# The feed-forward norm of an encoder block: roots on a diagonal, weights as ScalarE's scale, another order of the last sums

## The reference

```
mixed = concat([attention, convolution])
h  = h + mixed @ w_out[0]
hn = rmsnorm(h, ffn_norm_g)          # h * rsqrt(mean(h*h) + 1e-6) * g
g, u = hn @ w_gate, hn @ w_up        # 1024 -> 2816
h  = h + (silu(g) * u) @ w_down
out = rmsnorm(h, final_norm_g)[16:]
```

## Time and profile before

| | |
|---|---|
| runs | 1173.94, 1174.21, 1174.76 us; median 1174.21 |
| profiled execution | 1174.17 us |
| its span, first to last instruction | 1172.4 us |
| busy: TensorE, VectorE, POOL, ScalarE | 1151.2, 693.5, 451.2, 435.7 us |
| mean granted clock of TensorE | 0.998 |

### The profile page before, as it was taken

One profiled execution on the slowest core, in us unless ns is written; L12 is line 12 of the kernel. 1 busy time (PEld: TensorE's weight loads), 2 busy tenths in 40 slices (PEclk: granted clock), 3 DMA queues, 4 the chain that ended last, 5 costly groups with the idle time before them and its releaser, 6 DMA issues.

```text
span 1172.4 us, 15242 instructions
## 1 busy us (share of the span) xinstructions
PE 1151.2 (98%) x5890; PEld 986.8 (84%) x5890; DVE 693.5 (59%) x757; ACT 435.7 (37%) x875; POOL 451.2 (38%) x356
## 2 busy tenths in 40 slices
PE   9999999999999999989999999999999999999997
PEld 5899899899999888867888888888888888888886
DVE  5339898888898646694444445353435353534347
ACT  6321553533737644454141413132322222232323
POOL 4116000000000013267474646556564647473822
PEclk9999999999999999999999999999999999999999
DMA  7204312113026011122030202121212121212114
GB/s 265 81 10 100 71 48 72 38 49 85 13 54 227 19 37 54 36 72 62 13 102 5 87 22 73 36 72 36 72 37 72 37 72 36 72 37 72 37 36 162
DMA packets 70911, 75.69 MB, mean 65 GB/s; under 512 B 11513, under 2 KB 60149, under 8 KB 70840
## 3 DMA queue, kind: packets, MB, share of 16 engines
q1 hardware_dynamic: 69656, 72.60, 20.0%
q10 hardware_dynamic: 1184, 2.13, 0.5%
HBM read 64.13 MB, written 6.32 MB: 60 GB/s over the span
## 4 chain that ended last, share of the span: by engine, by line
PE 69%; DVE 5%; POOL 3%; issue 2%; ACT 0%; POOLq 0%; DVEq 0%; ACTq 0%
PE ps L1820 31%; PE ps L1841 20%; PE ps L1771 8%; PE ps L1631 6%; DVE gq L1298 3%; PE ps L1704 2%; POOL wa_lo L639 1%; DVE acc L1213 1%; PE ps L1689 1%; PE ps L1677 1%; POOL wb_lo L639 1%; DVE wo_lo L1236 0%; PE ps L1784 0%; PE ps L1754 0%; PE ps L1747 0%
## 5 line engine op out<-in xcount | busy, mean ns | idle before, releaser
L1486 DVE TENSOR_TENSOR mix<-ps,mix 128x512 f32<-128x512 f32 x176 | 121.7, 691 | 137.4 <-PE ps L1841 137.4
L1213 DVE SCALAR_TENSOR_TENSOR acc<-u_pad,par,acc 128x1024 f32<-128x1024 f32 x116 | 144.4, 1292 | 1.5 <-ACT acc L830 1.4
L1841 PE MATMUL ps<-wd_hi,act_hi 128*128 128x512 f32 x352 | 137.0, 389 | 0.3 <-DVE act_lo L1475 0.3
L1841 PE MATMUL ps<-wd_lo,act_hi 128*128 128x512 f32 x352 | 136.9, 389 | 0.0
L1841 PE MATMUL ps<-wd_hi,act_lo 128*128 128x512 f32 x352 | 136.9, 389 | 0.0
L625 POOL TENSOR_SCALAR ln_var<-bn 128x1 f32<-128x1 f32 x8 | 3.6, 450 | 338.7 <-DVE bn L1335 338.7
L1631 PE MATMUL ps<-hn_hi,wp_hi 128*128 128x348 f32 (+2 forms) x352 | 118.4, 336 | 0.0
L1631 PE MATMUL ps<-hn_lo,wp_hi 128*128 128x348 f32 (+2 forms) x352 | 117.6, 334 | 0.0
L1631 PE MATMUL ps<-hn_hi,wp_lo 128*128 128x348 f32 (+2 forms) x352 | 117.5, 334 | 0.0
L639 POOL TENSOR_TENSOR wa_lo<-raw,wa_hi 128x512 fp32r<-128x512 f32 x44 | 61.8, 1406 | 142.5 <-ACT wa_hi L1002 142.5
L1051 ACT ACTIVATE act_f<-ps 128x512 f32<-128x512 f32 x22 | 13.1, 598 | 246.1 <-PE ps L1820 246.1
(11 more groups left out here) (187 smaller groups left out, 2644.8 us busy)
## 6 DMA issues: line engine op xcount, KB each, us to landing
raw<-in_w_gate SPq DMA_DIRECT2D x11, 1024.0 KB, 5.3
raw<-in_w_up SPq DMA_DIRECT2D x11, 1024.0 KB, 5.3
wd_f<-in_w_down SPq DMA_DIRECT2D x11, 1024.0 KB, 4.8
raw<-in_w_in SPq DMA_DIRECT2D x16, 512.0 KB, 3.8
xin<-in_x SPq DMA_DIRECT2D x8, 512.0 KB, 10.4
wo_raw<-in_w_out SPq DMA_DIRECT2D x4, 1024.0 KB, 9.5
mix<-in_x SPq DMA_DIRECT2D x8, 512.0 KB, 3.4
out<-ost SPq DMA_DIRECT2D x7, 512.0 KB, 2.6
```

What stands on the lines that cost most here:

```text
L1213: dve.scalar_tensor_tensor(out=acc[:, j % 2, :], in0=u_pad[:, p % 2, j:j + L], scalar=par[:, p, j:j + 1], in1=acc[:, j % 2, :], op0=ALU.mu ...
L1486: dve.tensor_tensor(hrow, ps[:, TB + n % 4, :], hrow, ALU.add).then_inc(d_added, 1)
L1841: last = pe.matmul(ps[:, TB + n % 4, :], a[s][:, t, i * P:(i + 1) * P], w_[m][:, t, dh * BANK:(dh + 1) * BANK], start=(t == 0 and s == m = ...
```

## The change

POOL's `h_root(i)` now also multiplies the identity by the root of each token into `h_diag`, in two buffers. `transpose_h` multiplies the row of h itself, as stationary operand, by that diagonal: an f32 matmul for each block in place of a transpose. `norm_h` is gone. The weights of the norm lie in `g2c`, one column a block, and `evac_h` copies the banks in eight instructions with them as scale. `square_h` waits for its own last sum in place of the transposes. The slots 4 and 5 change places. `weight_sum(0,5)` and `weight_hi(0,5)` go ahead, to the last iteration of the tiles; `h_root(7)` goes ahead of the weight sums; `evac_h(7)` and `hi_h(7)` go ahead of `weight_hi(0,6)` and `(0,3)`, with `t_high` of T1 now ahead of all three; the sums T1 and T3 of tiles 6 and 7 alternate.

```diff
-             ("g2b", [P, D], F32)],
+             ("h_diag", [P, 2, P], F32)],
+        g2c = keep("g2c", [P, KD], F32)
-        FIRST_SLOT = [0, 1, 2, 0, 5, 2, 4, 0, 3, 5, 1, 2, 4, 3]
+        FIRST_SLOT = [0, 1, 2, 0, 4, 2, 5, 0, 3, 4, 1, 2, 5, 3]
-        SLOT = FIRST_SLOT + [(0, 5, 1, 2, 4, 3)[n % SLOTS] for n in range(len(LATER))]
+        SLOT = FIRST_SLOT + [(0, 4, 1, 2, 5, 3)[n % SLOTS] for n in range(len(LATER))]
-                  + [(t, i) for t in ("T1", "T3", "T2", "T4") for i in (6, 7)])
+                  + [(t, i) for i in (6, 7) for t in ("T1", "T3")] + [(t, i) for t in ("T2", "T4") for i in (6, 7)])
-            sp.dma_start(g2b[:, :], ffn_norm_g[0].partition_broadcast(P)).then_inc(g2_loaded, 16)
+            sp.dma_start(g2c[:, :], ffn_norm_g[0].rearrange("(k p) -> p k", p=P), allow_slow_non_contiguous=True).then_inc(g2_loaded, 16)
@@ POOL, h_root(i)
+                pool.wait_ge(h_rstd, i + 1)
+                if i >= 2:
+                    pool.wait_ge(ht_ready, i - 1)
+                pool.tensor_scalar(h_diag[:, i % 2, :], ident[:, :], rstd[:, n:n + 1], None, ALU.mult).then_inc(h_diag_ready, 1)
@@ POOL, loop over the tiles
+                if i == TILES - 1:
+                    pool.wait_ge(ms_used, TILES)
+                    weight_sum(0, 5)
                 if i >= 1:
                     h_root(i - 1)
@@ POOL, behind it
+            h_root(TILES - 1)
             pool.wait_ge(wo_ready, 2 * TILES)
-            weight_sum(0, 5)
             weight_sum(0, 6)
-            h_root(TILES - 1)
             weight_sum(0, 3)
@@ ScalarE
             def square_h(i):
                 act.wait_ge(h_ready, 2 * (i + 1))
                 if i:
-                    act.wait_ge(ht_ready, i)
+                    act.wait_ge(h_sumsq, i)
...
             def evac_h(i):
                 c = slice((i % 4) * P, (i % 4 + 1) * P)
+                if i == 0:
+                    act.wait_ge(g2_loaded, 16)
                 act.wait_ge(ht_ready, i + 1)
-                act.activation(hn2f[:, i // 4, :, c],
-                               ps[:, TB:TB + 2, :].rearrange("p b (k t) -> p (b k) t", k=4), ACT.Copy).then_inc(hf_ready, 1)
+                for k in range(KD):
+                    act.activation(hn2f[:, i // 4, k, c], ps[:, TB + k // KH, (k % KH) * P:(k % KH + 1) * P], ACT.Identity,
+                                   scale=g2c[:, k:k + 1], bias=zeros[:, 0:1]).then_inc((hf_low, hf_high)[k // KH], 1)
...
                     act.wait_ge(ms_used, TILES)
-                    t_high("T1", 4, 6)
+                    weight_hi(0, 5)
                     square_h(i)
                 if i >= 1:
                     evac_h(i - 1)
                     hi_h(i - 1)
-            t_high("T2", 4, 6)
...
-            weight_hi(0, 5)
+            t_high("T1", 4, 6)
+            evac_h(TILES - 1)
+            hi_h(TILES - 1)
             weight_hi(0, 6)
             weight_hi(0, 3)
-            evac_h(TILES - 1)
-            hi_h(TILES - 1)
+            t_high("T1", 6, 8)
+            t_high("T2", 4, 6)
             weight_hi(0, 4)
-            t_high("T1", 6, 8)
             copy(0, 1)
             t_high("T2", 6, 8)
             weight_hi(1, 2)
@@ VectorE: norm_h and its calls are gone; t_sum waits for the halves it reads
-                    dve.wait_ge(hf_ready, i + 1)
+                    dve.wait_ge(hf_low, KH * (i + 1))
...
             residual(TILES - 1)
             for t in ("T2", "T4"):
                 t_sum(t, 5)
-            t_low(1, "T1", 4, 6)
-            norm_h(TILES - 1)
             t_sum("T1", 6)
             lo_h(TILES - 2)
+            t_sum("T3", 6)
+            t_low(1, "T1", 4, 6)
+            lo_h(TILES - 1)
             t_sum("T1", 7)
-            lo_h(TILES - 1)
-            t_sum("T3", 6)
-            t_low(3, "T1", 6, 8)
+            t_low(2, "T1", 6, 8)
             t_sum("T3", 7)
@@ TensorE
             def transpose_h(i):
-                pe.wait_ge(hn_ready, i + 1)
-                pe.wait_ge(hf_ready, i)
+                pe.wait_ge(h_diag_ready, i + 1)
+                pe.wait_ge(hf_low, KH * i)
+                pe.wait_ge(hf_high, KH * i)
+                hrow = mix[:, i, :, :].rearrange("p k t -> p (k t)")
                 for k in range(KD):
-                    last = pe.transpose(ps[:, TB + k // 4, (k % 4) * P:(k % 4 + 1) * P],
-                                        xn2[:, k * P:(k + 1) * P], ident[:, :])
+                    last = pe.matmul(ps[:, TB + k // 4, (k % 4) * P:(k % 4 + 1) * P],
+                                     hrow[:, k * P:(k + 1) * P], h_diag[:, i % 2, :], start=True, stop=True)
                 last.then_inc(ht_ready, 1)
```

More of the change, by code:

```diff
@@ L164, in hybrid_block @@
             [("mix", [P, TILES, KD, P], F32)])
-        (wp_hi, wp_lo, ms_hi, ms_lo, xn2, g2b, wb_hi, wb_lo, sil, skip_4, wb_f) = region(
+        (wp_hi, wp_lo, ms_hi, ms_lo, xn2, h_diag, wb_hi, wb_lo, sil, skip_4, wb_f) = region(
             "region4", 4 * KD * P,
@@ L255, in hybrid_block @@
         xres_loaded = [sem("xres_loaded0"), sem("xres_loaded1")]
-        h_sumsq, h_var, h_rstd, hn_ready = sem("h_sumsq"), sem("h_var"), sem("h_rstd"), sem("hn_ready")
-        ht_ready, hf_ready, hhi_ready, hlo_ready = sem("ht_ready"), sem("hf_ready"), sem("hhi_ready"), sem("hlo_ready")
+        h_sumsq, h_var, h_rstd, h_diag_ready = sem("h_sumsq"), sem("h_var"), sem("h_rstd"), sem("h_diag_ready")
+        ht_ready, hf_low, hf_high, hhi_ready, hlo_ready = sem("ht_ready"), sem("hf_low"), sem("hf_high"), sem("hhi_ready"), sem("hlo_ready")
         t_summed, thi_ready, tlo_ready = sem("t_summed"), sem("thi_ready"), sem("tlo_ready")
@@ L979, in evac_h @@
                 c = slice((i % 4) * P, (i % 4 + 1) * P)
+                if i == 0:
+                    act.wait_ge(g2_loaded, 16)
                 act.wait_ge(ht_ready, i + 1)
-                act.activation(hn2f[:, i // 4, :, c],
-                               ps[:, TB:TB + 2, :].rearrange("p b (k t) -> p (b k) t", k=4), ACT.Copy).then_inc(hf_ready, 1)
+                for k in range(KD):
+                    act.activation(hn2f[:, i // 4, k, c], ps[:, TB + k // KH, (k % KH) * P:(k % KH + 1) * P], ACT.Identity,
+                                   scale=g2c[:, k:k + 1], bias=zeros[:, 0:1]).then_inc((hf_low, hf_high)[k // KH], 1)
             def hi_h(i):
                 c = slice((i % 4) * P, (i % 4 + 1) * P)
-                act.wait_ge(hf_ready, i + 1)
+                act.wait_ge(hf_high, KH * (i + 1))
                 if i < 4:
+                    act.wait_ge(hf_low, KH * (i + 1))
                     act.activation(b0_hi[:, :, c], hn2f[:, 0, :, c], ACT.Copy).then_inc(hhi_ready, 1)
@@ L1349, in residual @@
                     dve.tensor_tensor(hrow[:, c], ps[:, (PJ, PV)[i % 2] + dh, :], hrow[:, c], ALU.add).then_inc(h_ready, 1)
[L1351 to L1357, removed]
             def lo_h(i):
@@ L1377, in t_sum @@
                     dve.wait_ge(t_summed, t_done("T1", i))
+                    dve.wait_ge(hf_high, KH * (i + 1))
                     dve.tensor_tensor(b12, b22, b12, ALU.subtract).then_inc(t_summed, 1)
@@ L1408, in _ @@
                     ln_normalise(i + 1)
-                if i >= 1:
-                    norm_h(i - 1)
                 if i + 2 < TILES:
@@ L1873, in _ @@
             product(0, 6)
-            pe.wait_ge(hf_ready, TILES)
+            pe.wait_ge(hf_low, KH * TILES)
+            pe.wait_ge(hf_high, KH * TILES)
             product(1, 5)
```

## The result

| | before | changed |
|---|---|---|
| median | 1174.08 us (1173.22 to 1174.76, 4 runs) | 1185.59 us (1185.37 to 1186.83, 4 runs) |
| profiled execution, span | 1174.17, 1172.4 us | 1186.83, 1185.1 us |

The ratio is 1.0102, with a 95% interval of 1.0088 to 1.0115: the changed kernel is 1% slower, 11.5 us. The forecast was 1183.4, in a range of 1178 to 1187. The changed kernel's profiled execution was its longest run, 1.2 us over the median, so the traces differ by 12.7 us of span, where the medians differ by 11.5.

The account below looks back on a forecast made before the run. TensorE, busy for 98% of the span, was taken to bound the kernel. Matmuls for transposes in tiles 0 to 4 (4.6 us), waits at `ln_backward` (1.2) and the hand-over (3.4) summed to +9.2 us: 1183.4 us, range 1178 to 1187.

Parts of the forecast that it names:

- rival G: Transposes: a block's matmul costs four transposes, +2.6 us a tile in place of 0.92, giving 1196 us; chance 0.01.
- The wait at `ln_backward`: Tiles 0 to 3: the longer evacuation delays the normalise `ln_backward` waits for, 0.3 us four times, 1.2 us.
- `transpose_h(6)`: Hand-over: TensorE waits for tile 6's diagonal from POOL, a new wait of 0.7 us.
- (0,3): Hand-over product: its weights come behind `evac_h(7)`, so it starts at 23.3 and not 19.67, a 3.6 us wait.
- The load: Up block's load, issued by SP after POOL's `weight_lo(0,4)`: 26.4 us after `transpose_h(5)` starts, landing 5.4 us later.
- (1,2): Hand-over product needing the up block: starts at 33.9 where TensorE is free at 28.75, a 5.1 us wait.
- B: Evacuation pieces cost less than their model: about 1179.6 us, 1178 if the clock holds; chance 0.17.
- C: VectorE and POOL slow one another in the new order: 1187 us; chance 0.10.
- A: The forecast: heavier transposes, loads and weights gated by `evac_h(7)`; 1183.4 us, own range 1180.5 to 1186; chance 0.60.
- D: The order fills the hand-over's waits: all 10.5 us go and 7.35 come, 1171.0 us; chance 0.04.
- E: Half of the hand-over's waits go: 1174.2 + 7.35 - 6 = 1175.5 us; chance 0.05.
- F: `transpose_h`: the matmul of a block is one instruction after all, 1176.0 us; chance 0.03.

Follow-up runs that it names:

- row_transposes: Changed kernel with transposes of the rows of h in place of the diagonal matmuls, the root left out of the result: 1177.97 us.
- plain_matmul: Kernel before with `transpose_h` as f32 matmuls of the normed row with the identity: 1179.82 us, ratio 1.0047.
- eight_pieces: Kernel before with `evac_h` as eight 128x128 instructions, scale of ones and bias of zeros: 1180.45 us, ratio 1.0053.
- bank_copies: Changed kernel with `evac_h` as two copies, one of each bank, in place of eight scaled pieces, norm weights left out: 1181.09 us.
- weights_ahead: Changed kernel with the high parts of (0,6) and (0,3) made ahead of `evac_h(7)`: 1186.04 us.
- load_ahead: Changed kernel with the high parts of (0,6), (0,3) and also (0,4) made ahead of `evac_h(7)`: 1181.91 us, ratio 1.0064.
- order_alone: Kernel before with the change's order and slots alone; transposes, `norm_h` and one-piece evacuation stay: 1175.71 us, ratio 1.0016.
- low_parts_apart: order_alone plus (0,6), (0,3), (0,4) high parts ahead of `evac_h(7)`, `lo_h(7)` and `weight_hi(1,2)` earlier, POOL's `weight_lo(0,4)` before a held-back `weight_lo(0,5)`: 1175.82 us.

## Why the prediction held, step by step

The chain came as forecast, and its parts nearly so. What was off was almost always too small: the traces differ by 12.7 us where the sum said 9.2. That the medians differ by only 11.5, and the error comes out as 2.2 us and not 3.5, is owed to which execution was profiled.

- **The matmuls.** +0.91 us a tile against +0.92, 7.6 us in row_transposes against 7.35. The count of instructions of another plain f32 matmul in the trace of before gave this, and it is most of what made the sign certain. The rule of a factor of four, rival G, does not hold here: it is 1.78 to 0.87.
- **The wait at `ln_backward`.** An iteration grew by 1.27 to 1.31 us for tiles 0 to 3, 0.91 of it the matmuls: 0.36 to 0.40 a tile, forecast 0.3. The evacuation took 2.90 us, as forecast. Up to `transpose_h(5)` the changed kernel is 6.36 us behind (5.8). Of that, 0.3 was there at the first `transpose_h` already; its start lies anywhere from 423.18 to 424.03 in six traces (before, after, plain_matmul, eight_pieces, bank_copies, row_transposes), so 0.3 is no more than these traces differ by.
- **`transpose_h(6)`**: idle 1.39 us, forecast 0.7. The diagonal takes 0.60 us on POOL, twice my figure, and the root 1.02 beside VectorE's work where I had 0.55. These are mis-sized terms.
- **(0,3)**: 3.57 us, forecast 3.6. **The load**: 27.7 us after `transpose_h(5)`'s start, forecast 26.4. **(1,2)**: 5.16 us idle, forecast 5.1. The trace has the chain as it was walked, and bank_copies, weights_ahead and load_ahead move its pieces as it says. The idle times fit better than the starts: (0,3) starts at t = 24.4 where the walk had 23.3, and (1,2) at 35.3 where it had 33.9, mostly from `transpose_h(6)` and from `weight_lo(0,4)`, 1.97 us and not 1.64.
- **After (1,2)** the step was too small by 1.3 us: the lower clock lasted 6.9 us and not 3.4, so (1,2) lost 2.2 and not 1.7, and one wait of 0.40 stayed, where none was forecast. In all, the hand-over lost 6.13 us against 3.4 forecast. These 2.7 us, with the 0.6 up to `transpose_h(5)`, are nearly all of the 3.5 us between the traces and the sum.
- **Rivals.** B falls (pieces cost 0.35 us each). C, the price of VectorE and POOL beside one another, is real: the root and `weight_lo(0,4)` took 0.5 and 0.3 us more than in the walk, each beside VectorE. The measured time lies nearer to C's 1187 than to A's 1183.4, but these two explain 0.8 of the 2.7 us, and no run has the change without them. It is also the likeliest reason why the reordered kernels did not gain, but that is argued and not shown. D and E, the order filling the waits, fall: order_alone is slower than before. F falls with the 128 instructions.
- **Slips in the working** that did not decide: TensorE's waits between 487.29 and 549.40 are seven, not six. The factor between the two forms is 1.79 / 0.87 = 2.06. D and E leave out the 1.2 us at `ln_backward` that stands in the sum, and half of 10.5 us, for E, is 5.25 and not 6.

Open: what the removed `norm_h` was worth, and the last 0.4 us of the 1.3 after (1,2), which may be restarts after a wait.

## What to carry to other kernels

Before folding a scale into a transpose, count the instructions of a plain f32 matmul and of a transpose in a trace: here it is two against one on the engine that bounds the kernel, to save work on engines that had time. When a copy out of the banks is cut in pieces, reckon it by its latency where something waits in order behind it, not by the idle time of its engine. In a hand-over between two stages, find the instruction that the next load waits for and follow it through every queue; moving another one alone only moves the wait.

## What was not expected of the hardware

- A low clock can last twice 3.4 us. It did in the changed kernel (0.57 over 8 us), where it fell during a wait of 5.2 us. In order_alone it was low for as long around a wait of 6.3 us (0.84, 0.50 and 0.81 in the three windows of 4 us from 512 to 524). In the kernel before one spell of 3.4 us followed waits of 1.2 and 1.8; in plain_matmul no spell followed waits of 1.4, 0.9 and 2.3. In eight_pieces the lower clock added more (2.7 us) than the longer waits beside it (1.9).
- VectorE and POOL stretch each other a good deal: 0.68 to 1.75 us for a 128x512 f32 subtraction, 1.3 to 1.7 or 2.2 for POOL's. In low_parts_apart the stretch moved to other instructions and did not go away.
